# Attention value rows turned by VectorE from a DRAM copy, in pairs of tiles, in place of TensorE transposes

## The chip, the cores and the metric

The kernel runs on one core of one Trainium2 chip. The metric is the device time in microseconds of one execution; lower is better. A run is timed from outside; the profile of one execution gives the span of its instructions, which is a little shorter.

## The reference, cut to what matters

One encoder layer for two groups of streams: one new stream of 16 meta and 256 prompt tokens, and eight running streams of 16 tokens each, which have a cache of 256 past keys and values. That makes 400 token columns, and the kernel keeps all three groups (sample tokens, prompt tokens, meta tokens) in one matrix of them.

```
aq, ak, av, mq, mk, mv, mi, mf, mo = split(rms_norm(x) @ w_in)    # 2048 -> 56 tiles of 128 columns
s   = q @ k^T * DQK**-0.5 + relative bias, masked by chunk       # two maps per head, 4 heads
w   = softmax(s[0]) - lam * softmax(s[1])
o   = rms_norm(w @ v, subln_g)                                    # v: new rows and, for a stream, the cached ones
hm  = chunkwise mLSTM of mq, mk, mv with states C, n, m
x   = x + concat(o, hm * sigmoid(mo)) @ w_out
y   = x + square(relu(rms_norm(x) @ w_up)) @ w_down
```

Outputs are y, the new keys (`k_prompt`, `k_sample`), the new values (`v_prompt`, `v_sample`) and the new mLSTM states. All arithmetic is fp32; the large products are made of three fp32r products each (weights and activations split in a high and a low part).

## The kernel before

**Tiles of the projections.** The first product is done in tiles of 128 output columns, numbered t = 0 to 47. In each the 2048 inputs are summed in 16 steps, four in a quarter q = 0 to 3, and each step is three matmuls over the 400 (or 384) token columns: activation high by weight high (L540), low by high (L541), high by low (L542). A quarter is 12 matmuls. SyncE loads raw weights two half tiles at a time (`load_tile`), ScalarE copies a quarter into `w_hi` (L511), VectorE subtracts it into `w_lo` (L520), and TensorE waits for `w_lo`. There are four quarter buffers, so these two engines are at most a tile ahead of TensorE. Behind each tile VectorE reads the sum from `acc` and scales it (`scaled`, L1440). Tiles 0 to 7 are queries, 8 to 15 keys, 16 to 23 the attention's values (`av`, into `m1`, features on the partitions), 24 to 31 the mLSTM's queries and keys, 32 to 47 its values and gates.

**What runs beside them.** Every engine's program is written out tile by tile, and after each quarter it does the side work that a plan gives to that slot. `att_plan` makes the plan of the attention; slot s = 4·(t − 24) + q stands behind quarter q of tile t. All engines walk through the same plan, each doing its part of a step: `scores` (TensorE's products, then VectorE's row maximum, L1631), `exp` (ScalarE), `weights` (VectorE), `turn` (TensorE), `out`, and so on. The steps are, for each of four heads or stream pairs j, two query blocks of the prompt, ("p", j, 0) and ("p", j, 1), and the pair j of running streams. A prompt step begins at slot 4 + 8·(2j + i); the pair's last scores come at slot 16, 32, 48, 64.

**The key tiles of the streams.** The cached keys of stream b come in by strided loads (`load_keys`, `kc`), and VectorE turns them in four pieces into `kT` (L1702) at slots 4 + 8b to 7 + 8b. TensorE's `first_scores` (at slot 8 for stream 0) waits for the fourth piece, and so do its scores at slot 16 for stream 1 (`blocks_turned`).

**The new keys for the output.** `ko` (at slots 1, 5, 9, ..., 29) turns a tile of new keys in two VectorE transposes (L1679, L1681), and ScalarE issues four stores of it in the slots behind (`ko_store`).

**The value rows, which the change is about.** The attention needs `v` with tokens on the partitions (`av_rows`). At quarter 0 of tile t (18 to 23) and at slots 0 and 4, `turn_av` makes four TensorE transposes of an `m1` tile into a PSUM bank (L2177), and VectorE copies them out, the 128 x 384 part (L1599) and the 16 rows of the tail (L1600). That is eight times 4 transposes and 2 copies.

**GpSimd's queue.** GpSimd issues, in this order: the cached values of streams 0 and 1 (`load_values`, into the two buffers of `vc`); 16 loads of mLSTM state blocks through DRAM, each waiting for the next tile to have been scaled (`state_blocks`); the stores of the value rows to the outputs, after all eight tiles are turned; then the cached values of streams 2 to 7, in twos, each two behind the `out` step of the pair before; then the mLSTM's value blocks (`load_v_blocks`, 13 DMAs per head into `kv_blk`, in pieces of 32 x 32 that VectorE then transposes), and more. TensorE's `out` step of pair 0 (slot 20) waits for the cached values of both its streams.

## Time and profile before

| | us |
|---|---|
| median of 3 runs | 1732.14 (1731.73 to 1732.16) |
| the profiled execution's own time | 1731.3 |
| its span | 1729.5 |

```profile
PE 1723.6 (100%) x8450; PEld 1467.3 (85%) x8450; DVE 906.2 (52%) x1681; ACT 654.3 (38%) x1224; POOL 392.1 (23%) x558
PE   9999999999999999999999999999999999999999
DVE  5634676556687666545433554343465334456333
DMA  7685469999898676665334565344556444556542
q0 software_dynamic: 24976, 66.98, 14.4%
```

The first line gives each engine's busy time, its share of the span and its instructions (PE is TensorE's matmuls, PEld its weight loads, DVE is VectorE, ACT ScalarE, POOL GpSimd). The next three cut the span into 40 slices of 43 us and give the busy share in tenths: TensorE is busy throughout, VectorE about half, and the DMA engines are near full in slices 7 to 13, some 260 to 560 us, where the attention and the mLSTM run. The last one is GpSimd's DMA queue (packets, MB, share of the 16 DMA engines). TensorE's granted clock is 0.9 or more of full speed in every slice.

### The profile page before, as it was taken

The numbers are of one execution on the slowest core, as the hardware profiler recorded it, in microseconds if no ns is written. First come the engines' busy times: TensorE is split into PE (matmuls) and PEld (weight loads), VectorE is DVE, ScalarE is ACT, GpSimd is POOL, SyncE is SP. The second block draws the span as 40 slices with busy tenths as digits, with TensorE's granted clock in tenths as the row PEclk, the third lists the DMA queues.
The fourth block names the chain that finished last, engine by engine and source line by source line (L and its number), as shares of the span: only waits on it lengthen the run. The fifth ranks groups of instructions, "written<-read, shape, count | busy, mean of one in ns | idle before, by whom it ended". The sixth has DMA issues, their size and how long they took to land.

```text
span 1729.5 us, 24656 instructions
## 1 busy us (share of the span) xinstructions
PE 1723.6 (100%) x8450; PEld 1467.3 (85%) x8450; DVE 906.2 (52%) x1681; ACT 654.3 (38%) x1224; POOL 392.1 (23%) x558
## 2 busy tenths in 40 slices
PE   9999999999999999999999999999999999999999
PEld 8999999999997788888888888888888888888887
DVE  5634676556687666545433554343465334456333
ACT  5323754444354444333333333323333332333332
POOL 3321010002351253434000343000343100234100
PEclk9999999999999999999999999999999999999999
DMA  7685469999898676665334565344556444556542
GB/s 192 175 194 144 130 143 243 214 204 229 224 269 268 156 215 199 179 182 166 126 123 133 161 177 186 122 128 128 159 166 182 140 132 121 162 166 171 172 144 97
DMA packets 295746, 295.08 MB, mean 171 GB/s; under 512 B 97004, under 2 KB 202540, under 8 KB 295644
## 3 DMA queue, kind: packets, MB, share of 16 engines
q1 hardware_dynamic: 255606, 222.91, 46.7%
q0 software_dynamic: 24976, 66.98, 14.4%
q10 hardware_dynamic: 15062, 3.86, 1.1%
q8 instruction: 61, 1.00, 0.2%
q14 instruction: 41, 0.34, 0.1%
HBM read 261.44 MB, written 38.01 MB: 173 GB/s over the span
## 4 chain that ended last, share of the span: by engine, by line
PE 98%; DVE 1%; DMA 0%; issue 0%; ACT 0%; ACTq 0%; DVEq 0%
PE bank L680 9%; PE bank L681 9%; PE bank L639 9%; PE bank L638 9%; PE bank L640 9%; PE bank L679 9%; PE acc L540 8%; PE acc L541 8%; PE acc L542 8%; PE bank L2072 3%; PE ssb L638 2%; PE ssb L639 2%; PE ssb L640 2%; PE ssb L679 2%; PE ssb L680 2%; PE ssb L681 2%
## 5 line engine op out<-in xcount | busy, mean ns | idle before, releaser
L520 DVE TENSOR_TENSOR w_lo<-raw,w_hi 128x512 fp32r<-128x512 f32 x768 | 537.0, 705 | 753.8 <-ACT w_hi L511 753.2
L511 ACT ACTIVATE w_hi<-raw 128x512 fp32r<-128x512 f32 x768 | 482.4, 631 | 958.3 <-PE acc L542 195.5
L540 PE MATMUL acc<-a_hi,w_hi 128*128 128x400 f32 (+1 forms) x768 | 267.9, 349 | 0.2 <-DVE w_lo L520 0.2
L541 PE MATMUL acc<-a_lo,w_hi 128*128 128x400 f32 (+1 forms) x768 | 262.9, 342 | 0.0
L542 PE MATMUL acc<-a_hi,w_lo 128*128 128x400 f32 (+1 forms) x768 | 262.3, 342 | 0.0
L680 PE MATMUL bank<-w_lo,a_hi 128*128 128x512 f32 x640 | 253.0, 395 | 0.0
L681 PE MATMUL bank<-w_hi,a_lo 128*128 128x512 f32 x640 | 252.6, 395 | 0.0
L639 PE MATMUL bank<-w_lo,x2g_hi 128*128 128x512 f32 x640 | 252.4, 394 | 0.0
L640 PE MATMUL bank<-w_hi,x2g_lo 128*128 128x512 f32 x640 | 252.2, 394 | 0.0
L638 PE MATMUL bank<-w_hi,x2g_hi 128*128 128x512 f32 x640 | 252.1, 394 | 0.0
L679 PE MATMUL bank<-w_hi,a_hi 128*128 128x512 f32 x640 | 252.1, 394 | 0.0
L619 POOL DMA_DIRECT2D u_turned<-m x192 | 124.0, 653 | 550.1 <-DVE m L2015 548.6
L540 PEld LDWEIGHTS acc<-a_hi,w_hi 128*128 128x128 f32 x768 | 144.2, 188 | 4.8 <-issue 3.4
L542 PEld LDWEIGHTS acc<-a_hi,w_lo 128*128 128x128 f32 x768 | 144.8, 189 | 0.0
L541 PEld LDWEIGHTS acc<-a_lo,w_hi 128*128 128x128 f32 x768 | 144.3, 188 | 0.3
L681 PEld LDWEIGHTS bank<-w_hi,a_lo 128*128 128x128 f32 x640 | 120.7, 189 | 27.7
L640 PEld LDWEIGHTS bank<-w_hi,x2g_lo 128*128 128x128 f32 x640 | 120.5, 188 | 27.8
L680 PEld LDWEIGHTS bank<-w_lo,a_hi 128*128 128x128 f32 x640 | 120.4, 188 | 28.0
L679 PEld LDWEIGHTS bank<-w_hi,a_hi 128*128 128x128 f32 x640 | 120.4, 188 | 27.7
L639 PEld LDWEIGHTS bank<-w_lo,x2g_hi 128*128 128x128 f32 x640 | 120.3, 188 | 27.6
L638 PEld LDWEIGHTS bank<-w_hi,x2g_hi 128*128 128x128 f32 x640 | 120.3, 188 | 27.6 <-issue 0.2
L932 POOL TENSOR_TENSOR a_lo<-stage,a_hi 128x384 fp32r<-128x384 f32 x64 | 71.8, 1153 | 121.2 <-ACT a_hi L1347 121.2
(358 smaller groups left out, 1812.1 us busy)
## 6 DMA issues: line engine op xcount, KB each, us to landing
raw<-in_w_up SPq DMA_DIRECT2D x128, 512.0 KB, 3.8
raw<-in_w_down SPq DMA_DIRECT2D x128, 512.0 KB, 3.8
raw<-in_w_in SPq DMA_DIRECT2D x94, 512.0 KB, 4.9
raw<-in_w_out SPq DMA_DIRECT2D x32, 512.0 KB, 5.6
u_turned<-m POOLq DMA_DIRECT2D x192, 64.0 KB, 3.0
stage<-u_turned POOLq DMA_DIRECT2D x16, 768.0 KB, 6.2
vc<-in_cache_v POOLq DMA_DIRECT2D x32, 256.0 KB, 7.1
kc<-in_cache_k SPq DMA_DIRECT2D x128, 64.0 KB, 3.2
```

What stands on the lines that cost most here:

```text
L511: e.activation(w_hi[:, q], raw[:, slot, 4 * (q % 2):4 * (q % 2) + 4, :], ACT.Copy).then_inc(hi_ready, 1)
L520: e.tensor_tensor(w_lo[:, q], raw[:, slot, 4 * (q % 2):4 * (q % 2) + 4, :], w_hi[:, q].bitcast(F32), ALU.subtract).then_inc(lo_ready, 1)
L540: e.matmul(out, w_hi[:, q, kk], hi[:, k, at], start=k == 0, stop=False, skip_group_check=True)
L541: e.matmul(out, w_hi[:, q, kk], lo[:, k, at], start=False, stop=False, skip_group_check=True)
L542: last = e.matmul(out, w_lo[:, q, kk], hi[:, k, at], start=False, stop=k == KT - 1, skip_group_check=True)
L619: e.dma_start(bass.AP(tensor=u_turned_d.tensor, offset=(b % 2) * 4 * P * 3 * P + Y_STARTS[r] - META + 32 * a, ap=[[3 * P, 32], [32 * 3 * P ...
L638: e.matmul(to, x2g_hi[:, k, rows], hi_w, start=k == 0, stop=False, skip_group_check=True)
L639: e.matmul(to, x2g_hi[:, k, rows], lo_w, start=False, stop=False, skip_group_check=True)
L640: last = e.matmul(to, x2g_lo[:, k, rows], hi_w, start=False, stop=k == KT - 1, skip_group_check=True)
L679: e.matmul(out, a_hi[:, k, rows], hi_w, start=k == 0, stop=False, skip_group_check=True)
L680: e.matmul(out, a_hi[:, k, rows], lo_w, start=False, stop=False, skip_group_check=True)
L681: last = e.matmul(out, a_lo[:, k, rows], hi_w, start=False, stop=k == KT - 1, skip_group_check=True)
```

## The change

1. The TensorE transposes of the value tiles and VectorE's copies of them out of PSUM are gone. GpSimd stores each `m1` value tile to a DRAM tensor `av_d`, and after two of them `av_back` loads the pair back with 13 DMAs, in pieces of 32 features x 8 x 32 tokens, into the second buffer of `vc`, which is renamed `av_blk` for the purpose and has room for two pairs' halves (n % 2). VectorE then makes token rows of a pair by two transposes of 32 x 32 blocks (`turn_av`). The four pairs are turned behind quarter 1 of tiles 21 and 23, and at slots 3 and 14.
2. The cached values of stream 1 are loaded into that buffer only when all four pairs are turned, and the stores of the value rows go behind the loads of all streams.
3. The new keys are turned and stored every 6 slots, not every 4.
4. Some semaphores are shared between waits (`gw_padded` becomes `consts`, and the like); the waits remain as they were.

```
-AV_AHEAD = T_M - T_AV - 2
+KEYS_EVERY = 6
+AV_TURNS = {(5, 1): 0, (7, 1): 1}
...
-    plan += [(4 * (j - AV_AHEAD), "av", j) for j in range(AV_AHEAD, 8)] + [(4 * j + 1, "ko", j) for j in range(8)]
-    plan += [(4 * j + 2 + g, "ko_store", (j, g)) for j in range(8) for g in range(4)]
+    plan += [(3, "av", 2), (14, "av", 3)] + [(KEYS_EVERY * j + 1, "ko", j) for j in range(8)]
+    plan += [(KEYS_EVERY * j + 2 + g, "ko_store", (j, g)) for j in range(8) for g in range(4)]
...
+        av_d = nc.dram_tensor("av_d", [8, P, TOK], F32).ap()
...
+            av_blk = vc[:, 1].rearrange("p x (r i t) -> p x r i t", i=8, t=32)
...
-            for b in range(2):
-                load_values(b)
+            load_values(0)
+            e.memset(av_blk[0:32, :, 3, :, TAIL:32], 0.0).then_inc(S("wt_padded"), 1)
...
+            def av_back(n):
+                e.wait_ge(S("av_out"), 16 * 2 * (n + 1))
+                if n >= 2:
+                    e.wait_ge(S("av_turned"), n - 1)
+                else:
+                    e.wait_ge(S("wt_padded"), 2)
+                at = 2 * n * P * TOK
+                for j in range(4):
+                    rows = slice(32 * j, 32 * j + 32)
+                    for r in range(3):
+                        dma(av_blk[rows, n % 2, r], bass.AP(tensor=av_d.tensor, offset=at + STARTS[r] + 32 * j,
+                                                            ap=[[TOK, 32], [32 * TOK, 8], [1, 32]]), f"av_in{n % 2}")
+                dma(av_blk[0:32, n % 2, 3, :, 0:TAIL], ...)
...
             for n in range(16):
                 ... state_blocks as before ...
+                if n >= 8:
+                    if n > 8:
+                        e.wait_ge(S("av_out"), 16 * (n - 8))
+                    dma(av_d[n - 8], m1[:, n - 8], "av_out")
+                if n in (10, 12, 14, 15):
+                    av_back((n - 9) // 2)
-            read_out(e, *[("av", j) for j in range(8)])
+            e.wait_ge(S("av_turned"), 4)
+            load_values(1)
+            for b in range(2, BD):
+                done(e, ("o", b // 2 - 1))
+                load_values(b)
             ... the three stores of av_rows ...
-            for b in range(2, BD):
-                done(e, ("o", b // 2 - 1))
-                load_values(b)
...
-            def take_av(n):
-                b = take(e, ("av", n))
-                cs = slice(n * P, (n + 1) * P)
-                e.tensor_copy(av_rows[:, 0:3, cs], b[:, 0:3 * P].rearrange("p (r n) -> p r n", n=P))
-                taken(e.tensor_copy(av_rows[0:TAIL, 3, cs], b[0:TAIL, 3 * P:4 * P]), ("av", n))
+            def turn_av(n):
+                cs = slice(n * DV, (n + 1) * DV)
+                e.wait_ge(S(f"av_in{n % 2}"), 16 * 13 * (n // 2 + 1))
+                e.transpose(av_rows[0:32, 3, cs], av_blk[0:32, n % 2, 3].rearrange("p i t -> p (i t)"))
+                e.transpose(av_rows[:, 0:3, cs],
+                            av_blk[:, n % 2, 0:3].rearrange("p r i t -> p r (i t)")).then_inc(S("av_turned"), 1)
...
-            def turn_av(n):
-                e.wait_ge(acc_free, T_AV + n + 1)
-                turn_rows(("av", n), m1[:, n])
```

VectorE's program from the scaling of the last value tile (`m`, tile 23) to the first prompt step's scores (slots 0 to 4), before:

```order
L1440 TENSOR_TENSOR m<-acc,rstd_x 128x400
L520 TENSOR_TENSOR w_lo<-raw,w_hi 128x512
L1599 COPY av_rows<-bank 128x3x128
L1600 COPY av_rows<-bank 16x128
L520 TENSOR_TENSOR w_lo<-raw,w_hi 128x512
L1684 MEMSET w_new 128x128
L1685 MEMSET q_pad 128x8x16
L1679 STREAM_TRANSPOSE ko<-zt 128x288
L1681 STREAM_TRANSPOSE ko<-zt 128x128
L520 TENSOR_TENSOR w_lo<-raw,w_hi 128x512 x2
L1440 TENSOR_TENSOR m<-acc,rstd_x 128x384
L520 TENSOR_TENSOR w_lo<-raw,w_hi 128x512
```

Two more copies of `av_rows` follow there, and then the scores (L1631). The same stretch in the changed kernel, where L519 is the `w_lo` line, L1462 the scaling, L1621 and L1622 the transposes of `turn_av`, L1654 the scores:

```order
L1462 TENSOR_TENSOR m<-acc,rstd_x 128x400
L519 TENSOR_TENSOR w_lo<-raw,w_hi 128x512 x2
L1707 MEMSET w_new 128x128
L1708 MEMSET q_pad 128x8x16
L1702 STREAM_TRANSPOSE ko<-zt 128x288
L1704 STREAM_TRANSPOSE ko<-zt 128x128
L519 TENSOR_TENSOR w_lo<-raw,w_hi 128x512 x2
L1462 TENSOR_TENSOR m<-acc,rstd_x 128x384
L1621 STREAM_TRANSPOSE av_rows<-vc 32x256
L1622 STREAM_TRANSPOSE av_rows<-vc 128x3x256
L519 TENSOR_TENSOR w_lo<-raw,w_hi 128x512
L1654 ISA s_sb,smx<-bank,bias_p 128x144
```

Four copies have left this stretch and two transposes, of a pair, have come, ahead of the last `w_lo`. VectorE at slots 12 to 15 of the changed kernel, where the key tiles of stream 1 are turned (L1725 is `kT`; before, the same rows stand there without the two of `av_rows`):

```order
L1725 STREAM_TRANSPOSE kT<-kc 128x2x8x32
L519 TENSOR_TENSOR w_lo<-raw,w_hi 128x512
L1702 STREAM_TRANSPOSE ko<-zt 128x288
L1704 STREAM_TRANSPOSE ko<-zt 128x128
L1725 STREAM_TRANSPOSE kT<-kc 128x2x8x32
L519 TENSOR_TENSOR w_lo<-raw,w_hi 128x512
L1621 STREAM_TRANSPOSE av_rows<-vc 32x256
L1622 STREAM_TRANSPOSE av_rows<-vc 128x3x256
L1725 STREAM_TRANSPOSE kT<-kc 128x2x8x32
```

The pair's two transposes stand between the second and the third key piece. GpSimd's DMAs of the changed kernel from the last stores of value tiles on:

```order
L728 DMA state_blocks<-in_state_C 32x64x32
L728 DMA av_d<-m 128x400
L728 DMA vc<-av_d 32x8x32 x12
L728 DMA vc<-av_d 32x8x16
L728 DMA state_blocks<-in_state_C 32x64x32
L728 DMA av_d<-m 128x400
L728 DMA vc<-av_d 32x8x32 x12
L728 DMA vc<-av_d 32x8x16
L728 DMA vc<-in_cache_v 32x2x1024 x28
L728 DMA out<-av_rows 128x1024
```

The first four rows are the reload of the third pair (tiles 4 and 5), behind the store of tile 6; before, only the two rows of `state_blocks` stood there, and `out<-av_rows` came right behind them.

## Rows read from the trace of the kernel before

**Rows 1.** The page: the chain of waits that ended last, by engine
```profile
PE 98%; DVE 1%; DMA 0%; issue 0%; ACT 0%; ACTq 0%; DVEq 0%
```
**Rows 2.** TensorE's waits: line, for whom, us in total, times, longest
```profile
PE bank L2072 <- DVE kT L1702: 0.4, 1, 0.4
```
**Rows 3.** Timeline of TensorE at tile 18: start us, us, line, operation [idle before]
```profile
184.90 0.34 PE L542 MATMUL acc<-a_hi,w_lo 128*128 128x400 f32 x1
185.08 0.60 PE L2177 MATMUL bank<-ident,m 128*128 128x128 f32 x4
...
185.71 0.34 PE L541 MATMUL acc<-a_lo,w_hi 128*128 128x400 f32 x1
185.89 0.35 PE L542 MATMUL acc<-a_hi,w_lo 128*128 128x400 f32 x1
```
**Rows 4.** The transposes' line L2177: ns min/median/max, first and last start
```profile
L2177 PE MATMUL bank<-ident,m x32: 270/272/273, 185.1 to 253.7; 128*128 128x128 f32 x24, 128*16 128x128 f32 x8
```
**Rows 5.** Timeline of VectorE from the scaling of tile 22 to slot 8
```profile
239.09 0.57 DVE L1440 TENSOR_TENSOR m<-acc,rstd_x 128x400 f32<-128x400 f32 x1
...
254.65 0.68 DVE L520 TENSOR_TENSOR w_lo<-raw,w_hi 128x512 fp32r<-128x512 f32 x1
255.25 0.55 DVE L1599 COPY av_rows<-bank 128x384 f32<-128x384 f32 x1
...
255.91 0.28 DVE L1631 CUSTOM_DVE_ANT_0 s_sb<-bank,bias_p 128x144 f32<-128x144 f32 x1
...
260.03 0.47 DVE L1679 STREAM_TRANSPOSE ko<-zt 128x288 f32<-128x288 f32 x1
...
260.61 0.67 DVE L1702 STREAM_TRANSPOSE kT<-kc 128x512 f32<-128x512 f32 x1
...
263.57 0.70 DVE L1702 STREAM_TRANSPOSE kT<-kc 128x512 f32<-128x512 f32 x1
```
**Rows 6.** Timeline of TensorE at slot 8
```profile
262.94 1.02 PE L2072 MATMUL ssb<-av_rows,wT 128*128 128x256 f32 x4
264.32 0.64 PE L2072 MATMUL bank<-kT,q_pad 128*32 128x256 f32 x8 [0.36 <-DVE kT L1702]
```
**Rows 7.** Tile kv_blk: instructions with ns min/median/max, and time to landing
```profile
L729 POOL DMA_DIRECT2D kv_blk<-kv_d x52: 615/618/667, 420.2 to 519.2; - x52
L1916 DVE STREAM_TRANSPOSE kv_rows<-kv_blk x4: 556/558/559, 449.0 to 556.4; 32x384 f32<-32x384 f32 x4
L1917 DVE STREAM_TRANSPOSE kv_rows<-kv_blk x4: 1323/1323/1323, 449.5 to 556.9; 128x1152 f32<-128x1152 f32 x4
...
DMA to landing us min/median/max: 2.5/5.6/10.1
```
**Rows 8.** Timeline of GpSimd: the state blocks behind tile 22
```profile
240.24 1.05 POOL L729 DMA_DIRECT2D state_blocks<-in_state_C  x1 [9.16 <-DVE m L1440]
```
**Rows 9.** Tile state_blocks: time to landing of its DMAs
```profile
DMA to landing us min/median/max: 4.0/4.6/9.7
```
**Rows 10.** Timeline of VectorE at slots 12 to 15, stream 1
```profile
278.01 0.17 DVE L1641 RECIPROCAL smx<-smx 128x2 f32<-128x2 f32 x1 [1.19 <-ACT s_sb L1187]
...
284.01 0.71 DVE L1702 STREAM_TRANSPOSE kT<-kc 128x512 f32<-128x512 f32 x1
```
**Rows 11.** Timeline of TensorE at slots 16 and 20
```profile
285.33 1.07 PE L2072 MATMUL bank<-kT,q_pad 128*32 128x256 f32 x16
...
295.81 1.93 PE L2072 MATMUL ssb<-vc,wT 128*32 128x256 f32 x32
```
**Rows 12.** Tile vc: time to landing of the cached values' DMAs
```profile
DMA to landing us min/median/max: 4.2/7.1/11.0
```
**Rows 13.** Timeline of VectorE at slot 38, stream 4
```profile
349.70 0.69 DVE L520 TENSOR_TENSOR w_lo<-raw,w_hi 128x512 fp32r<-128x512 f32 x1 [0.44 <-ACT w_hi L511]
```
**Rows 14.** The page's DMA issues: KB each, us to landing
```profile
out<-av_rows POOLq DMA_DIRECT2D x1, 1024.0 KB, 9.1
```

More of the change, by code:

```diff
@@ L249, in plan_banks @@
     for _, what, n in ATT_PLAN:
-        if what == "av":
-            u.add(("av", n), (2, 4)[n % 2])
-        elif what == "first_scores":
+        if what == "first_scores":
             u.add(("s", STEPS[n], 0), 0)
@@ L1192, in att_work @@
                         if n == 0:
-                            e.wait_ge(S("wt_padded"), 2)
+                            e.wait_ge(S("wt_padded"), 3)
                         if is_pair(step):
@@ L1570, in qk_norm @@
                 cols = pair_cols(u)
-                if q == 0 and u >= 2:
-                    take_av(u - 2)
+                if (u, q) in AV_TURNS:
+                    turn_av(AV_TURNS[u, q])
                 elif q == 2 and u + 1 < 8:
@@ L1673, in att_work @@
                     if what == "av":
-                        take_av(n)
+                        turn_av(n)
                     elif what == "ko":
@@ L1683, in att_work @@
                     elif what == "mask":
-                        e.memset(w_new[:], 0.0).then_inc(S("w_new_zero"), 1)
-                        e.memset(q_pad[:, :, 1], 0.0).then_inc(S("w_new_zero"), 1)
-                        e.wait_ge(S("w_new_zero"), 2)
-                        e.wait_ge(S("bias_masked"), 2)
-                        e.wait_ge(S("lam_ready"), 1)
+                        e.memset(w_new[:], 0.0).then_inc(S("pads_zero"), 1)
+                        e.memset(q_pad[:, :, 1], 0.0).then_inc(S("pads_zero"), 1)
+                        e.wait_ge(S("pads_zero"), 2)
+                        e.wait_ge(S("bias_masked"), 3)
+                        e.wait_ge(S("lam_prod"), 2)
                     elif what == "key_blocks":
@@ L1883, in enter @@
                 e.memset(expo[:, EXPO_TAIL:], 0.0).then_inc(S("pads_zero"), 1)
-                e.wait_ge(S("pads_zero"), 3)
+                e.wait_ge(S("pads_zero"), 5)
                 e.memset(v_rows[:, 0:3, DV:DVX], 1.0)
@@ L1895, in enter @@
                     last = ts(swm[:, h], bmask[:], cols[:, 1, 0, h:h + 1], None, ALU.mult)
-                last.then_inc(S("swm_made"), 1)
-                e.wait_ge(S("swm_made"), 1)
+                last.then_inc(S("seq_paired"), 1)
+                e.wait_ge(S("seq_paired"), 3)
                 read_out(e, "nT")
@@ L2158, in qk_sums @@
                 u = t - T_AV
-                if q == 0 and u >= 2:
-                    turn_av(u - 2)
-                elif q == 1:
+                if q == 1:
                     if u == 0:
-                        e.wait_ge(S("consts"), 4)
+                        e.wait_ge(S("consts"), 5)
                     e.wait_ge(S("n_low"), u + 1)
@@ L2251, in att_work @@
                     yield slot
-                    if what == "av":
-                        turn_av(n)
-                    elif what == "first_scores":
+                    if what == "first_scores":
                         first_scores(STEPS[n])
```

14 lines of the change are left out of this document (7 added, 7 removed).

## Prediction

> **What bounds the kernel now.** I read the page first: the chain that ended last is TensorE's for 98% of the span [rows 1]. So TensorE sets the end, and every other engine matters only where TensorE waits for it. Then the table of TensorE's waits: in the stretch that the change touches it has one entry, 0.4 us for the key tiles that VectorE turns [rows 2]. The timeline shows where: at slot 8 TensorE has done its products with the value rows at 262.94, and could go on with stream 0's keys, but the fourth key piece begins on VectorE at 263.57 and takes 0.70, so TensorE begins at 264.32 after 0.36 of idling [rows 5, 6]. What TensorE gives up is thus worth its full length, provided that nothing then comes too late for it.
>
> **What TensorE loses.** The weight matmuls follow each other at 0.18 us (185.71 to 185.89). From 184.90 to 185.71 stand one turn of four transposes and two such steps: 0.81 − 0.36 = 0.45 us a turn, switching back to the weight products included [rows 3]. Eight turns go: −3.6 us. A transpose by itself lasts 272 ns [rows 4], but most of that overlaps the next one. The Trainium skill, "TensorE: Matmul & The Clock Gate", Part 4: PE-mode transpose, gives about 275 ns for one in a kernel's context, and the trace agrees on that length; counted by it, 32 transposes would be 32 × 275 ns = 8.8 us, an estimate from that page. Start to start they cost 0.45 us for four, and that is what I sum.
>
> **VectorE, slots 0 to 4.** Here the stretch from the scaling of tile 23 to slot 8 is almost one block of VectorE work. Two takes go, each 0.66 us (255.25 to 255.91) [rows 5]: −1.32. One turn of a pair comes, 128 x 768 and 32 x 256 elements. Neither is in the trace. Nearest are 128 x 512 at 0.70 [rows 5] and 128 x 1152 at 1.32, and for the small one 32 x 384 at 0.56 [rows 7]; a line through the first two gives 0.95 for 768, the small one in proportion 0.4, less 0.1 of overlap between neighbours: 1.25. Its bounds are 0.9 (the 0.70 and half of the 0.56, overlapping) and 1.88 (both upper rows). VectorE's work is then 0.07 us shorter, but TensorE arrives 2 × 0.45 = 0.9 earlier, as it has two turns less (slots 0 and 4). The fourth key piece is late already, so all of the difference is waited: +0.8 us. The `ko` that moves from slot 5 to slot 7 (0.58 us, 260.03 to 260.61) [rows 5] stays ahead of that piece and changes nothing there.
>
> **The new wait at slot 3.** VectorE now waits for the reload of value tiles 4 and 5. Queued behind this wait are a `w_lo`, the first prompt step's scores and weights, and all four key pieces of stream 0, on which TensorE waits. GpSimd's issue of the state blocks behind tile 22 stands at 240.24 and takes 1.05 [rows 8]; one store, taken as 0.62 like a reload DMA, and 13 reloads at 0.618 [rows 7] follow. The last one is issued at 240.24 + 1.05 + 0.62 + 12 × 0.618 = 249.3. Landing took 2.5 to 10.1 with a median of 5.6 for the like pieces of `kv_blk` [rows 7], and 4.0 to 9.7 with 4.6 for the state blocks in this stretch [rows 9]. I take 5.1, between the medians: 254.4. VectorE would be there at 254.65 − 0.66 (tile 6's take is gone) − 0.45 (TensorE has one turn less since tile 22) = 253.5. The wait is 0.9 us; with the ends 2.5 and 10.1 it is 0 or 5.9. As the fourth key piece has no spare, TensorE pays it whole: +0.9. Tile 0 to 3's reloads are issued at least as early against quarter 1 of tiles 21 and 23, some 20 us after their issue begins, and cost nothing unless landings are double the longest seen. The fourth pair has until slot 14, over 20 us after its issue.
>
> A rule of the Trainium skill speaks against the reload: "DMA: Bandwidth & Descriptors", Specifications, wants at least 512 B a transfer and says that smaller ones are read, modified and written. The reload is in pieces of 128 B, as `kv_blk` is, so the landings of rows 7 have that price in them already; by the rule the reload sits nearer the late end.
>
> **VectorE, slots 12 to 15.** The fourth pair is turned between stream 1's key pieces. VectorE works without a pause from 278.01, where ScalarE frees it, to the end of the fourth piece at 284.01 + 0.71 = 284.72 [rows 10]. TensorE needs that at 285.33 [rows 11], and between the end of such a piece and its use lie 0.05 (264.27 to 264.32) [rows 5, 6]. So 0.56 are to spare and 1.25 come: +0.7 us (0.3 to 1.3 by the bounds of the turn). A `ko` stands at slot 13 in both versions.
>
> **What costs nothing, and under what cover.** The values of stream 1 are issued when VectorE has done the fourth pair, about 283.5; the last of four issues at some 0.53 is at 285.1, landing takes 7.1 in the median and 11.0 at most [rows 12], so 292.2 or 296.1, and the product begins at 295.81 [rows 11], a little later with the waits above. Spare: 3.6 us, −0.3 in the worst case. The `ko` that is now at slot 37 adds 0.58 to stream 4's pieces, but VectorE idles 0.44 for ScalarE behind it [rows 13]; the rest fits into the like of the 0.56 found for stream 1. The reloads keep GpSimd from its next state blocks by 8 us, three times; no one waits for these before slot 67. The early removal of four `vc` DMAs and of six other turns' copies frees VectorE and the DMA engines where TensorE waits for neither: 0. The stores of the value rows now stand behind stream 7's values; 9.1 us to landing [rows 14], and VectorE asks for them only at slot 67, over 30 us later. The renamed semaphores: 0.
>
> **Sum.** −3.6 + 0.8 + 0.9 + 0.7 = −1.2 us. The profiled execution took 1731.3, so 1730.1; the median stands 0.84 above it, which gives 1730.9.
>
> **The rivals.**
> - *No new wait.* If the reload lands at the early end and VectorE has slack that I don't see in slots 0 to 4 and 12 to 15, only −3.6 remains: 1728.5. For it: TensorE waits almost nowhere now. Against: the 0.36 of rows 6 show a late VectorE, and rows 10 and 11 leave 0.56 for 1.25.
> - *The reload is late, slower than before.* At slot 3 VectorE stands until the third pair has landed; at 10.1 us of landing that is 5.9 instead of 0.9. −3.6 + 0.8 + 5.9 + 0.7 = +3.8: 1735.9. It makes the kernel slower than before from a wait of 2.1 us on, a landing of 6.3. For it: at this time the key loads of stream 0 and `state_blocks` share the DMA engines, and one of the latter took 9.7. Against: in the stretch's medians it is 4.6.
> - *The value stores get in the way.* They now fall on the key loads of stream 7. If these are pushed back by half of the stores' 9.1 us, and all of that is waited for, +4.5: 1735.4. Against: stream 7's pieces are turned some 25 us after the stores start.
> - *The transposes are worth their length.* By the rows' 272 ns each, 32 × 0.272 = 8.7 in place of 3.6: 1725.8. Against: rows 3, start to start. This is what the page's 275 ns would give.
>
> **Chances.** My forecast 0.60 (own range 1729.6 to 1732.5), no new wait 0.18, reload late 0.12, stores 0.07, transposes worth their length 0.03. About 0.2%, 3.5 us, is what a measurement of this kernel can tell from no change, so faster means below 1728.7 and slower above 1735.6. No new wait is just at that line, and I count most of it as faster: 0.13 + 0.03 and a little of the forecast's tail, 0.18. Slower is half of the late reload and a part of the stores: 0.11. The same: 0.71. The range 1728.3 to 1734.6 reaches from "no new wait" into the late reload up to a wait of 4.6 us.
>
> **What would show it.** In the changed profile TensorE's line for value transposes is gone and a tile of 400 columns with quarter sums is 0.45 us shorter. TensorE waits for `kT` twice: about 2.1 us at slot 8 (0.4 + 0.8 + 0.9) and 0.7 at slot 16. VectorE's `av_rows` transposes take 0.95 and 0.4, and at slot 3 the line has about 0.9 us of idle time before it with the reload as its releaser. TensorE's `vc` products have no wait. A `kT` wait under 1 us in all would make it the first rival; one of 6 the second; a wait in the 400s the third; anything above 0.1 us for `w_lo` would be a cost that I have not seen.

## The result, and the profile after

| | us, median (lowest to highest, runs) | ratio, 95% interval |
|---|---|---|
| before | 1731.99 (1731.15 to 1732.36, 19) | |
| after | 1734.70 (1732.01 to 1736.70, 19) | 1.0016 (1.0009 to 1.0022) |
| predicted | 1730.9, range 1728.3 to 1734.6 | |

The forecast was 3.8 us too low, and the time lies just above its range. Two things are to be explained: the median, and a spread of 4.7 us where the kernel before had 1.2. The profiled execution took 1732.04 us, so it is one of the shortest, and doesn't show all of the loss. Its chain of waits, against [rows 1]:

```profile
PE 95%; DVE 2%; SPq 1%; issue 1%; ACT 0%; DMA 0%; ACTq 0%; POOL 0%; DVEq 0%; POOLq 0%
```

TensorE's waits, against [rows 2] (line, for whom, us in total, times, longest):

```profile
PE bank L2095 <- DVE kT L1725: 1.7, 2, 1.0
PE bank L637 <- issue: 1.4, 1, 1.4
PE bank L2102 <- ACT o_rows L1247: 0.6, 1, 0.6
```

The tile that answers to [rows 3] no longer has its step of 0.45 us (TensorE at tile 18; start us, us):

```profile
184.66 0.35 PE L539 MATMUL acc<-a_hi,w_hi 128*128 128x400 f32 x1
184.84 0.35 PE L540 MATMUL acc<-a_lo,w_hi 128*128 128x400 f32 x1
185.03 0.34 PE L541 MATMUL acc<-a_hi,w_lo 128*128 128x400 f32 x1
```

VectorE's turn of a pair, which no row of before showed, at slot 3, and its last key piece of stream 1, against [rows 5, 10]:

```profile
251.97 0.42 DVE L1621 STREAM_TRANSPOSE av_rows<-vc 32x256 f32<-32x256 f32 x1
252.33 0.92 DVE L1622 STREAM_TRANSPOSE av_rows<-vc 128x768 f32<-128x768 f32 x1
253.19 0.64 DVE L519 TENSOR_TENSOR w_lo<-raw,w_hi 128x512 fp32r<-128x512 f32 x1
...
282.93 0.69 DVE L1725 STREAM_TRANSPOSE kT<-kc 128x512 f32<-128x512 f32 x1
```

TensorE at slots 8 and 16, against [rows 6, 11]:

```profile
262.10 0.64 PE L2095 MATMUL bank<-kT,q_pad 128*32 128x256 f32 x8 [1.02 <-DVE kT L1725]
...
283.77 0.85 PE L2095 MATMUL bank<-kT,q_pad 128*32 128x256 f32 x12 [0.64 <-DVE kT L1725]
```

And the time to landing of the tile `vc`, now with the 52 reload transfers in it, against [rows 7, 9, 12]:

```profile
DMA to landing us min/median/max: 2.4/5.0/10.8
```

From these alone the kernel would be faster. To see where a lead is won or lost I set the start of one and the same product of TensorE (counted back from the last one) in each trace against the kernel before. Minus is ahead, plus behind. At 170 us nothing has been changed yet; what stands there is the difference between two executions.

```
us in the kernel before   170    258    300    417    432   1185   1300
after                    0.68  -2.87  -1.55  -1.55  -0.73  -0.80   0.74
```

So 3.55 us are won by 258 us and 1.32 given back at the two waits for `kT`. 0.82 go between 417 and 432 us, at the wait for `o_rows`, and 1.54 at 1191 us, where the last big loop jumps back. The prediction had neither of the last two. Every table of leads below is made in this way; a lead is that of one execution, so it is to be read beside the median.

### The profile page after: what moved, and what is told of

It reads as the page before. It is cut to its first block, busy times and chain, and to the rows that moved or that the text cites. A ratio compares the mean times of both kernels' runs of the same rounds, so it can differ in the third digit from the quotient of the medians.

```text
span 1730.2 us, 24637 instructions
## 1 busy us (share of the span) xinstructions
PE 1721.5 (99%) x8418; PEld 1464.6 (85%) x8418; DVE 905.8 (52%) x1673; ACT 653.3 (38%) x1224; POOL 426.2 (25%) x619
## 4 chain that ended last, share of the span: by engine, by line
PE 95%; DVE 2%; SPq 1%; issue 1%; ACT 0%; DMA 0%; ACTq 0%; POOL 0%; DVEq 0%; POOLq 0%
PE bank L679 9%; PE bank L680 9%; PE bank L638 9%; PE bank L637 9%; PE bank L639 9%; PE bank L678 9%; PE acc L539 7%; PE acc L540 7%; PE acc L541 7%; PE bank L2095 3%; PE ssb L637 2%; PE ssb L638 2%; PE ssb L639 2%; PE ssb L678 2%; PE ssb L679 2%; PE ssb L680 2%
## 5 line engine op out<-in xcount | busy, mean ns | idle before, releaser
L519 DVE TENSOR_TENSOR w_lo<-raw,w_hi 128x512 fp32r<-128x512 f32 x768 | 537.1, 705 | 756.8 <-ACT w_hi L510 753.4
```

What stands on the lines that cost most here:

```text
L519: e.tensor_tensor(w_lo[:, q], raw[:, slot, 4 * (q % 2):4 * (q % 2) + 4, :], w_hi[:, q].bitcast(F32), ALU.subtract).then_inc(lo_ready, 1)
```

## Experiments

Each kernel ran 11 times, and the kernel before 21 or 33 times beside each set of kernels (medians 1731.64 to 1731.96). The ratio is to that. These theories stood in turn: F, fetching of instructions at the jump back; W and P, TensorE's own waits or its lead; K, the spacing of the new keys' stores, or the waits for `kT`; S, the transfers that the change adds or moves into the stage from 240 to 430 us.

**1. The changed kernel again, and the place of the loop.** `a_again` is the changed kernel itself.

> The changed kernel once more, to see in the trace what one of its usual, longer executions holds; the profiled one before was among its shortest (1732.0 us, where the median is 1734.7). Theory F (fetch of instructions at TensorE's jump back in the last big loop): the first product of that loop's second turn comes late by 1.5 us and more, and the difference between executions is there. Theory W (waits in the attention stage): the two waits for kT (0.7 us each) and the wait for o_rows at 426 us are longer or more than in the first profile. Both: a median near 1734.7 us with a spread of 4 us.

1732.65 us (1730.23 to 1735.36), 1.0005 (0.9996 to 1.0014).

```
# a_pad72, behind each tile of T_AV to T_M - 1
+                for _ in range(9):
+                    e.nop()
# a_slot0 (slot 0, changed kernel) and b_slot184 (slot 184, kernel before)
-            with e.Fori(1, GROUPS - 1) as g:
+            with nc.Fori(1, GROUPS - 1, engines=[e.engine], head_slot={e.engine: 0}) as g:
```

> The changed kernel with 9 instructions that do nothing on TensorE after each of tiles T_AV to T_M - 1, 72 in all, so that everything behind them, the last big loop too, lies where it lay in the kernel before. Theory F: the loss in the loop is gone; what is left is -3.6 us for the turns, +1.4 for the two waits for kT and +0.7 at 426 us: about 1730.5 us, with a spread of 1 us as before. Theory W: nothing changes, near 1734.7 us with a spread of 4 us.

1733.95 us (1730.52 to 1738.04), 1.0011 (1.0002 to 1.0020). TensorE's instruction records number 9414, as in the changed kernel, and no trace of this case has a record of an instruction that does nothing. So it is not shown that the padding was executed, and this may be the changed code a third time. Either way its loop loses only 0.2 us, and the 1730.5 us that Theory F asks for then did not come.

> The changed kernel with TensorE's last big loop laid so that its first instruction is the first of a block of 256 that is fetched at once. Theory F: as with the padding, about 1730.5 us and a narrow spread, if the place of the loop's head alone decides. Theory W: near 1734.7 us.

1733.54 us (1731.34 to 1735.55), 1.0007 (0.9998 to 1.0016).

> The kernel before with TensorE's last big loop laid so that its first instruction is number 184 of a block of 256, where it lies in the changed kernel (72 instructions ahead of a boundary); nothing else is changed. Theory F: 1 to 5 us slower than the kernel before, with a spread of some 4 us. Theory W: as the kernel before, 1732.0 us.

1733.39 us (1731.60 to 1733.93), 1.0006 (0.9997 to 1.0015).

```
us in the kernel before   170    258    300    417    432   1185   1300
a_again                  0.46  -3.08  -1.70  -1.70   0.84   1.41   1.35
a_pad72                  0.20  -3.35  -2.03  -2.03   2.46   2.45   2.65
a_slot0                  0.15  -3.39  -2.01  -0.77   4.03   4.22   4.26
b_slot184                0.46   0.46   0.41   0.41   0.41   0.49   2.20
```

The part up to 300 us repeats to 0.2 us. The part from 300 to 432 doesn't: in four executions with the changed kernel's work it cost 0.8, 2.5, 4.5 and 6.0 us. That is the spread. The loop costs 1.7 us in `b_slot184`, and nothing in `a_again`, which is the same code as the profiled one that lost 1.5 there. In `b_slot184` the median rose with it, by 1.4 us. Theory F names a true loss, but not the main one. One more thing is to be kept in mind: the changed code itself gave medians of 1734.70 and 1732.65, 2.05 us apart. `a_again` shows what happens around 417 us. SyncE's issues, first of the kernel before, then of `a_again` (start us, us that the issue took):

```profile
393.29 0.37 SPq L488 DMA_DIRECT2D raw<-in_w_in  x1
393.70 11.56 SPq L1002 DMA_DIRECT2D kc<-in_cache_k  x8
405.31 0.49 SPq L488 DMA_DIRECT2D raw<-in_w_in  x1
405.85 6.26 SPq L1002 DMA_DIRECT2D kc<-in_cache_k  x8
412.16 0.49 SPq L980 DMA_DIRECT2D kv_d<-stage  x1
412.76 1.13 SPq L488 DMA_DIRECT2D raw<-in_w_in  x2
```

```profile
391.65 0.37 SPq L487 DMA_DIRECT2D raw<-in_w_in  x1
392.07 17.23 SPq L1024 DMA_DIRECT2D kc<-in_cache_k  x8
409.35 0.48 SPq L487 DMA_DIRECT2D raw<-in_w_in  x1
409.88 6.12 SPq L1024 DMA_DIRECT2D kc<-in_cache_k  x8
416.04 0.49 SPq L1002 DMA_DIRECT2D kv_d<-stage  x1
416.64 1.14 SPq L487 DMA_DIRECT2D raw<-in_w_in  x2
```

GpSimd loads streams 6 and 7's values just ahead of it, and now stores the value rows too (`a_again`):

```profile
387.81 3.63 POOL L728 DMA_DIRECT2D vc<-in_cache_v  x7 [0.23 <-issue]
391.43 1.81 POOL L728 DMA_DIRECT2D out<-av_rows  x3
```

Eight key issues take 17.2 us instead of 11.6, and the weight pieces queued behind them on SyncE come 4 us later. ScalarE waits for them, in the kernel before never, here (all waits from 240 to 440 us, then one of them, then TensorE behind it):

```profile
ACT w_hi L510 <- DMA raw<-in_w_in: 16.8, 6, 5.3
```
```profile
421.71 0.63 ACT L510 ACTIVATE w_hi<-raw 128x512 fp32r<-128x512 f32 x1 [5.32 <-DMA raw<-in_w_in]
```
```profile
428.79 0.44 PE L2102 MATMUL bank<-ident,o_rows 128*128 128x128 f32 x2 [1.46 <-ACT o_rows L1247]
```

The `o_rows` scaling stands behind that `w_hi` on ScalarE. So the wait is named after `o_rows`, but its cause is a late weight piece.

**2. The value stores and the spacing of the key stores.**

```
# a_early (b_late is the reverse move in the kernel before)
             load_values(1)
+            dma(v_sample..., av_rows[:, 0], "v_stored")        # and the two for vp
             for b in range(2, BD):
                 done(e, ("o", b // 2 - 1))
                 load_values(b)
-            dma(v_sample..., av_rows[:, 0], "v_stored")        # and the two for vp
# a_keys4
-KEYS_EVERY = 6
+KEYS_EVERY = 4
# a_early_turns: as a_early, and
-    plan += [(3, "av", 2), (14, "av", 3)] + ...
+    plan += [(9, "av", 2), (11, "av", 3)] + ...
```

> The changed kernel with the three stores of value rows issued ahead of the loads of streams 2 to 7 (some 283 us) and no more behind them (392 us); nothing else is changed. In four executions of the changed code the stretch from 417 to 432 us cost 0.8, 2.5, 4.5 and 4.8 us more than in the kernel before. Theory S (the stores behind stream 7's values hold up the weight and key loads that SP issues at the same time): that loss goes; what is left is what the changed kernel had gained at 400 us, 1.6 to 2.0 us, so about 1730.2 us, with a spread of 1 to 2 us from the jump back in the last big loop. Theory K (the wider spacing of new keys' stores, or the two waits for kT): nothing changes, 1732.6 to 1734.7 us with a spread of 4 us.

1734.26 us (1731.97 to 1737.24), 1.0014 (1.0005 to 1.0023).

> The kernel before with only the value rows' stores moved behind the loads of streams 2 to 7; TensorE still turns the values and VectorE copies them. Theory S: a loss of 1 to 5 us between 417 and 432 us, and the wider spread: 1733 to 1736 us. Theory K: 1732.0 us as before.

1731.67 us (1731.30 to 1732.78), 0.9999 (0.9990 to 1.0008).

> The changed kernel with new keys' stores at every fourth slot as before (KEYS_EVERY 4); the value stores stay behind the loads. Theory S: the loss from 417 to 432 us stays, 1732.6 to 1734.7 us. Theory K: the spacing of these stores was the cause, about 1730.5 us and a spread of 1 us.

1734.17 us (1731.45 to 1738.50), 1.0017 (1.0007 to 1.0026).

> As the first kernel of this call, and the turns of pairs 2 and 3 at slots 9 and 11 and no longer at 3 and 14, so that neither stands ahead of key blocks of streams 0 and 1 on VectorE. If the two waits for kT (0.7 us each above the kernel before) come from these turns: both go, and the time is 1.4 us below the first kernel's, about 1728.8 us. If they come from late key loads, they stay, at about 1730.2 us.

1735.66 us (1733.97 to 1738.20), 1.0021 (1.0012 to 1.0030).

```
us in the kernel before   170    258    300    417    432   1185   1300
a_early                 -0.06  -3.61  -2.30   4.74   4.74   4.71   4.90
b_late                   0.50   0.50   0.38   0.38   0.38   0.66   0.58
a_keys4                  0.53  -3.02  -1.71  -1.71   0.29   0.25   0.15
a_early_turns            0.80  -2.74   2.29   2.29   3.97   4.04   4.04
```

By the medians Theory S had failed twice. The leads of `a_early` say otherwise. With the stores at 283 us nothing is lost from 417 to 432, as expected; but 7.0 us are lost behind them, all of it between 300 and 320 us. With the stores some 8 us earlier still, 5.0 us are lost between 258 and 300. So a loss goes where the stores go; but `a_early_turns` also loses 1.7 us from 417 to 432, where it has no stores. `b_late` loses nothing there: its eight key issues take 14.07 us instead of 11.56, and the weight piece behind them lands just as it is wanted, so the stores alone use up the room that there is and no more. The spacing of the key stores is not needed for it: with the old spacing the loss at 432 stays. `a_early_turns` has no wait of 1 us at slot 8 any more (0.2 us for `kT` in all), so the turns at slots 3 and 14 do cause those waits.

**3. Stores left out, stores in a gap, and the rest of the change alone.**

```
# a_nostore (a_nostore_turns: and turns at slots 9 and 11)
-            dma(v_sample..., av_rows[:, 0], "v_stored")
+            dma(v_sample...[0:1], av_rows[0:1, 0], "v_stored") # likewise one row of each vp
# a_383_turns: turns at 9 and 11, stores inside the loop over b
+                if b == 6:
+                    e.wait_ge(S("blocks_turned"), 25)
+                    dma(v_sample..., av_rows[:, 0], "v_stored")    # and the two for vp
# b_rest (kernel before)
-            for b in range(2):
-                load_values(b)
+            load_values(0)
...
             read_out(e, *[("av", j) for j in range(8)])
+            load_values(1)                                     # value stores behind the loop
# ... and "ko" and "ko_store" at 6 * j for 4 * j
```

> The changed kernel without its value output: of the three stores of value rows one row each is left, at their place behind the loads of streams 2 to 7. Theory S (these 1.1 MB beside 2 MB of values, 1 MB of keys and the weights make the transfers of 387 to 416 us too long): SP's keys from 392 us take 18 us again as in the kernel before, and no more 22 to 24, the loss from 417 to 432 us is gone, and the time is 1730.0 us with a spread of 1 to 2. Theory P (TensorE, 2 us earlier, is too early for the transfers in any case): the loss stays at 1 us and more, 1732 us and up.

1731.21 us (1728.97 to 1732.70), 0.9995 (0.9986 to 1.0004).

> As the first of this call, with the turns of pairs 2 and 3 at slots 9 and 11. With early stores these turns took away the waits for kT (ledger at 270 us: 3.0 us ahead and not 2.4), but the stores then came at 275 us and the next stretch lost 5 us. If the stores alone did that, this one is 1.4 us below the first of this call: 1728.6 us. If the earlier load of stream 1's values does it (it follows the last turn), it loses some 3 us between 270 and 300 us: 1733 us.

1731.02 us (1729.15 to 1732.85), 0.9996 (0.9987 to 1.0005).

> The changed kernel with the whole value output stored at 383 us, in the gap between the keys of streams 5 and 6 and the values of stream 6 (GpSimd waits for the first key block of stream 6), and the turns of pairs 2 and 3 at slots 9 and 11. Theory S with room in that gap: within 1 us of the second kernel of this call. If the gap is too short (the values of stream 6 start 3 us later), the keys from 392 us take over 20 us again, and it is 2 to 4 us above that kernel.

1733.13 us (1731.14 to 1736.21), 1.0010 (1.0001 to 1.0019).

> The kernel before with all of the change but the way of the values: TensorE turns them and VectorE copies them as before; stream 1's values are loaded behind the last copy, new keys' stores stand at every sixth slot, and the value stores follow the loads of streams 2 to 7. Theory S: SP's keys from 392 us take 20 us and more, but TensorE doesn't wait, since here nothing has used up the slack of 1.9 us: 1732 us as before. If the order of transfers alone costs TensorE time: 1733 us and up, with a wide spread.

1732.11 us (1731.47 to 1733.54), 1.0002 (0.9993 to 1.0012).

```
us in the kernel before   170    258    300    417    432   1185   1300
a_nostore                0.64  -2.90  -1.57  -1.57  -1.57  -1.60  -1.69
a_nostore_turns          0.41  -3.13  -3.38  -2.61  -0.91  -0.93  -1.02
a_383_turns              0.45  -3.10  -3.40  -3.28  -0.08  -0.06  -0.14
b_rest                   0.45   0.45   0.34   0.34   2.09   2.01   2.25
```

Without the stores the loss of 417 to 432 is gone in the profile, and the median falls by 1.4 to 3.5 us against the changed kernel's three medians; the spread stays 3.7 us, and the profiled execution (1729.70 us) is 1.5 us below the median, so the others lose something that this trace doesn't show. With the turns at 9 and 11 the whole lead of 3.4 us reaches 300 us, but 2.5 us of it are lost by 432 even without stores. `b_rest` was the surprise: the kernel before, with TensorE as late as ever, loses 1.8 us by 432. This is its longest execution, though (1733.54 us); its median stands 0.4 us above that of the kernel before, which is no clear difference. The first eight of its sixteen key issues take 16.64 us, all sixteen reach from 394.0 to 416.7 us (in the kernel before from 393.7 to 412.1):

```profile
394.03 16.64 SPq L1002 DMA_DIRECT2D kc<-in_cache_k  x8
```

**4. The lead alone, and the added transfers alone.**

```
# b_noturns (kernel before): TensorE's turn_av goes, and in VectorE's take_av
-                b = take(e, ("av", n))
+                e.wait_ge(acc_free, T_AV + n + 1)
-                e.tensor_copy(av_rows[:, 0:3, cs], b[:, 0:3 * P]...)
+                e.tensor_copy(av_rows[:, 0:3, cs], m1[:, n, 0:3 * P]...)
# a_noreload (a_noreload_nostore: and the stores cut to one row each)
-                if n in (10, 12, 14, 15):
-                    av_back((n - 9) // 2)
             e.wait_ge(S("av_turned"), 4)
-            load_values(1)                                     # now behind load_values(0)
# ... and VectorE's turns wait for these values and for the stores to av_d
# a_noreload_v281: load_values(1) stays where it is, and the turns read a tile that is cleared
# a_split: stores as in a_383_turns, but v_sample's at b == 4 (blocks_turned 17); turns at 3 and 14
```

> The kernel before without TensorE's 32 transposes of the values; VectorE copies the same number of elements from the unturned tiles at the same places, so the values in the output and in the attention are not the reference's. No transfer is changed. Theory P (a lead of TensorE is lost at the weight pieces that land just in time, whatever the transfers): the lead of 3.6 us at 258 us shrinks to some 1.8 us by 330 or 420 us (the slack of before at tiles 33 and 41 is 1.8 and 1.9 us): 1730.1 us. Theory S (the pieces follow TensorE, and only added transfers make them late): the 3.6 us are kept, 1728.3 us, with a spread of 1 us.

1728.89 us (1728.43 to 1729.71), 0.9985 (0.9976 to 0.9994).

> The changed kernel without the 52 transfers that read the values back in blocks, and with stream 1's values loaded at the start, as before; VectorE turns what lies in that tile, so the values are not the reference's. Transfers that are left of the change: the stores of value tiles from 190 us, the spacing of new keys' stores, the value stores behind the loads. Theory S, shares added up: the wait for the weights at tile 33 goes (slack 1.8 us again), the one at tile 41 stays because of the value stores: some 1.5 us below the changed kernel, 1732 us. Theory P: as the changed kernel, 1733.5 us.

1730.84 us (1729.85 to 1732.45), 0.9994 (0.9985 to 1.0003).

> As the kernel before it in this call, and of the three value stores one row each is left. All that the change adds to the transfers from 240 to 420 us is gone. Theory S: 3.0 us and more of the lead are kept, less the 1.4 us that TensorE waits for kT: 1730.2 us with a spread of 1 us. Theory P: some 1731.2 us, as without the stores alone, with its spread of 4 us.

1729.81 us (1729.04 to 1730.39), 0.9989 (0.9980 to 0.9998).

> As a_noreload (the changed kernel without the 52 transfers that read the values back; 1730.8 us), but stream 1's values are loaded behind the last turn, near 281 us, as in the changed kernel. VectorE turns a cleared tile, so the values are not the reference's. If the reload alone took the room: 1730.8 us again. If the load at 281 us did: as the changed kernel, 1733 us and up. With both alike: about 1732 us.

1733.11 us (1730.65 to 1737.57), 1.0013 (1.0004 to 1.0022).

> The changed kernel, complete, with the value stores in two parts, each in a gap of SP's key loads: the sample rows at 340 us, the prompt rows at 383 us (GpSimd waits for the first key block of streams 4 and 6). Theory S with room in the gaps: as the kernel without the stores, 1731.2 us. If a store there only pushes the values of streams 4 and 6 into the key loads: 1733 us, as the kernel with all of it at 383 us.

1734.01 us (1731.90 to 1736.35), 1.0012 (1.0003 to 1.0021).

```
us in the kernel before   170    258    300    417    432   1185   1300
b_noturns                0.07  -3.48  -2.72  -2.73  -2.72  -2.49  -2.55
a_noreload               0.97  -2.58  -1.18  -1.18   0.10   1.24   1.16
a_noreload_nostore       0.40  -3.15  -1.84  -1.84  -1.84  -1.80  -1.51
a_noreload_v281          0.05  -3.50  -2.16  -2.16  -0.71  -0.71  -0.64
a_split                  0.77  -2.78  -1.42  -1.14   1.99   2.05   3.37
```

`b_noturns` decides between S and P: TensorE gets the same lead with no transfer changed, gives back 0.8 us at slot 8, keeps the other 2.7 through this stage and ends 2.55 ahead, and the kernel is 2.8 us faster with a spread of 1.3. Theory P falls. Its waits for the late key piece, against [rows 2, 6]:

```profile
PE ssb L2068 <- ACT wT L1205: 0.5, 1, 0.5
PE bank L2068 <- DVE kT L1698: 0.4, 1, 0.4
```

Taking the added transfers away brings the spread down step by step: 4.7 and 5.1 us in the changed kernel (7.5 in `a_pad72`), 2.6 without reload and with stream 1's values early, 1.35 without the stores as well. `a_noreload_v281` parts the first of these steps: with the reload gone but stream 1's values still at 281 us the median is 1733.1 again, 2.3 us above `a_noreload`. That is about as much as two medians of the changed code differ, so the size is rough; that the spread goes from 2.6 to 6.9 us with it says the same. So it seems to be less the reads of 128 bytes that cost, and more 1 MB of plain loads at a bad time. SyncE in `a_noreload`, then in `a_noreload_v281`:

```profile
285.06 6.19 SPq L1023 DMA_DIRECT2D kc<-in_cache_k  x8
291.29 2.55 SPq L487 DMA_DIRECT2D raw<-in_w_in  x2
...
302.27 11.57 SPq L1023 DMA_DIRECT2D kc<-in_cache_k  x8
```
```profile
285.14 9.63 SPq L1022 DMA_DIRECT2D kc<-in_cache_k  x8
294.82 1.12 SPq L487 DMA_DIRECT2D raw<-in_w_in  x2
...
301.29 13.82 SPq L1022 DMA_DIRECT2D kc<-in_cache_k  x8
```

The keys take 3.4 us longer, the two weight pieces are issued 3.5 us later, and so run into the 2 MB of values that GpSimd asks for at 296 us; the next keys take 2.3 us longer. How far ahead the pieces land shows where this ends (for the first half of a weight tile: us from landing to the start of `w_hi`, from the landing events; 0.02 is a piece that was waited for):

```
tile   before b_noturns a_noreload_nostore a_noreload a_noreload_v281 after a_again a_split
33      1.79    2.15         2.35             2.25         0.02        0.55   0.02    0.02
37      2.23    2.66         2.13             0.86         0.13        2.19   0.02    0.02
41      1.91    1.12         2.14             0.02         0.02        0.02   0.02    0.02
```

The kept traces join the two ends of this chain. Take in each the time of the eight key issues that begin near 392 us (in `a_early` at 398), and TensorE's loss from 417 to 432 us:

```
                     eight issues, us   loss, us
b_slot184                 10.2            0
a_half                    10.8            0
before                    11.6            -
a_noreload_nostore        11.9            0
a_early                   11.9            0
b_noturns                 12.6            0
a_nostore                 13.3            0
b_late                    14.1            0
after                     15.2            0.8
a_early_turns             15.2            1.7
a_nostore_turns           16.0            1.7
a_noreload                16.4            1.3
b_rest                    16.6            1.8
a_again                   17.2            2.5
a_pad72                   17.2            4.5
a_noreload_v281           17.3            1.5
a_split                   17.7            3.1
a_keys4                   17.8            2.0
a_383_turns               18.3            3.2
a_slot0                   20.6            4.8
```

Up to 14.1 us nothing is lost, from 15.2 us on always something. Neither the lead nor the value stores are needed for a loss (`b_rest`, `a_nostore_turns`), and neither does it alone (`b_noturns`, `b_late`).

`a_split` and `a_383_turns` did not test the gap that I had in mind: the wait for the key block let the stores go only at 346.4 and 391.9 us (`a_383_turns`: 389.7), right ahead of the values of streams 4 and 6, which they pushed back. ScalarE then waited 18.5 us for weights in `a_split`. Whether stores in a true gap (322 to 326, 340 to 345 us) cost less was not tried.

**5. A version that should keep half.** VectorE turns heads 0 and 1 by way of memory, TensorE turns tiles 4 to 7 as before; stores and key stores as before; stream 1's values behind the second turn.

```
# a_half (changed kernel)
-                if n in (10, 12, 14, 15):
+                if n in (10, 12):
                     av_back((n - 9) // 2)
+                if n == 13:
+                    e.wait_ge(S("av_turned"), 2)
+                    load_values(1)
# TensorE's turn and VectorE's take of tiles 4 to 7 as in the kernel before; KEYS_EVERY = 4
```

> A complete version made from both: heads 0 and 1 (value tiles 0 to 3) are stored, read back in blocks and turned by VectorE, which is done at 231 us, ahead of the key loads; TensorE turns tiles 4 to 7 as before. Stream 1's values are loaded at 232 us, the value stores come at 256 us and new keys' stores at every fourth slot, as in the kernel before. Theory S: no transfer is added between 240 and 430 us, so the lead of 4 x 0.45 = 1.8 us is kept, and the wait for kT is the 0.4 us of before: 1731.7 - 1.8 = 1729.9 us, with a spread of 1 us; faster than both. Theory P has fallen with b_noturns. If reads of 128 bytes at 200 and 221 us delay the state blocks or stream 0's keys instead: 1731.7 us and up.

1735.60 us (1733.22 to 1737.36), 1.0019 (1.0010 to 1.0028).

```
us in the kernel before   170    258    300    417    432   1185   1300
a_half                  -0.22  -2.02   1.37   1.37   1.37   1.80   5.69
```

1.80 us of lead at 258, as summed. Then 3.4 us are lost: I had put the second turn at 231 us, but quarter 1 of tile 23 is at 241, where stream 0's keys begin:

```profile
241.01 2.11 POOL L732 DMA_DIRECT2D vc<-in_cache_v  x4 [11.94 <-DVE av_rows L1630]
```
```profile
264.14 1.06 PE L2110 MATMUL bank<-kT,q_pad 128*32 128x256 f32 x8 [2.07 <-DVE kT L1740]
```

From 270 to 432 it then loses nothing, with the transfers of before in that stage. The miss fits Theory S, but what made this wait was not taken apart, and a gain did not come: no complete version that beats the kernel before was found. The other 3.9 us go at the jump back; the trace names a wait for 1.9 of them (below), and the rest is open.

## Why the prediction was wrong

**What TensorE loses, −3.6.** Right: 3.55 us between 170 and 258 us, and 3.5 to 3.6 in nearly every version without these turns. The rival by the length of a transpose (−8.7) is out, and with it the 275 ns of the Trainium skill ("TensorE: Matmul & The Clock Gate", Part 4: PE-mode transpose) as a price: the length is right (272 ns), the cost start to start is 0.44 for four.

**VectorE at slots 0 to 4, +0.8.** Right in kind and size: TensorE lost 0.6 between 258 and 270 us, and 0.8 in `b_noturns`, where the lead alone meets the late key piece. The turn takes 0.42 and 0.92, against 0.4 and 0.95.

**The new wait at slot 3, +0.9.** It was not there: the turn at 251.97 has no idle time before it. VectorE came 1.5 us earlier than summed (253.5), and the reload was in time all the same: its last transfer was issued at 246.9 us, not 249.3, and landed at 250.6, 3.7 us later and not 5.1.

**Slots 12 to 15, +0.7.** Right: 0.71. The wait for `kT` there is 0.64.

The three others give −2.1; the trace has −2.23 from 170 to 300 us. So up to 300 us the sum of −1.2 was right to 1.0 us, in the kernel's favour. The sum has no loss behind 300 us, and 1731.99 − 2.2 would have made 1729.8; the measured median is 4.9 us above that.

**What costs nothing, summed as 0.** This is the step that failed. I priced each moved transfer by its own landing against the moment when its own data are asked for: stream 1's values against their product, the value stores against slot 67. Both are in time, and TensorE never waits for a `vc` tile. What I left out is the work that shares the DMA engines and stands queued on SyncE: the key loads and, behind them, the weight pieces, which at tiles 33, 37 and 41 landed only 1.8, 2.2 and 1.9 us before use. TensorE lost 0.8 to 6.0 us from 300 to 432 us in four executions with the changed kernel's work, behind such pieces, and nothing where no transfer was changed (`b_noturns`). By medians, the value stores cost 1.0 us (1730.84 against 1729.81, nothing else added); stream 1's values at 281 us instead of the start, 2.3 us (1733.11 against 1730.84); the reload itself what the changed kernel's medians leave above 1733.11, −0.5 to 1.6 us. These shares are rough, since two medians of the same changed code lie 2.05 us apart, and they add up otherwise in another order: without the stores but with the rest the median is 1731.21. That transfers are the cause is shown; how it is divided among them is not.

**The rivals.** The third had the mechanism (the stores get in the way of stream 7's transfers), its size (+4.5; measured 0.8 to 6.0 at 432) and nearly the time, 1735.4; its sign, a wait in the 400s, is there. I gave it 0.07, because stream 7's keys had 25 us. What was late was the weight piece queued behind them. It is not the whole of it: a loss comes there without the stores too (`a_nostore_turns`). The late reload did not happen.

**The jump back, +1.5 in the profiled execution,** was in no term. It can come from where the loop's code lies, which the change shifts: laid there, the kernel before lost 1.4 us of median (`b_slot184`). But `a_again`, the same code, has none of it, and `a_noreload_nostore`, whose TensorE program is that of the changed kernel, has a median of 1729.81 us with a spread of 1.35, which leaves no room for such a loss in most executions. So it is a small part of the 4.9 us; why it comes in one execution and not in another is open.

## What to carry to other kernels

A transfer that is moved must be priced against what is queued beside and behind it, not against the use of its own data. Find, for the stage that it enters, the piece with the least time between landing and use (here weights with 1.8 us), and take that as the room that there is. When the median rises and the spread with it, compare where one and the same product stands in several executions: the part that repeats is the change's own work, the part that doesn't was, here, transfers in a stage where the DMA engines are busy all the time. And leave the work out first (as `b_noturns` did) to see what the idea is worth at most: 2.8 us here, of which no complete version kept any.

## What the runs showed of the hardware

**The DMA engines' share is near one before and after.** The share and GB/s (last two numbers) from 300 to 430 us, before and after:

```profile
300.00:430.00 130.00, 130.00 (x883) 120.80 (x882) 77.91 (x212) 56.98 (x171) 19.20 (x36) 1.00 0.98 217
```
```profile
300.00:430.00 130.00, 129.38 (x878) 119.66 (x876) 78.05 (x212) 55.57 (x167) 19.40 (x36) 1.00 1.00 229
```

The share was 0.98 before the change. Rows of this view belonged into the prediction, as a warning that added transfers may lengthen others. They don't give the price: the changed kernel moved 229 GB/s at 1.00, and `b_noturns` keeps its lead at 0.98.

**One issue in SyncE's queue can stand for long while GpSimd's transfers are moving.** GpSimd's 2 MB of values are under way at this time in the kernel before too, and there the longest of SyncE's eight key issues took 3.5 us, in `a_nostore` 4.1. With the value stores (1.6 MB in all, not the 1.1 MB of an expectation above) right behind the values the longest took 5.9 us in `a_again`, 7.1 in `b_late`, 7.9 in the changed kernel and 13.1 in `a_slot0`. But it also took 7.4 us in `a_nostore_turns` and 9.8 in `a_early_turns`, with no such stores there, so what sets the length is not shown.

**The jump back of TensorE's big loop.** At 1188 us, TensorE's sequencer ran its next instruction 3.5 us after the branch in the kernel before and 3.4 to 3.8 in `a_again`, `a_pad72`, `a_slot0` and `a_nostore`. It took 5.0 us in the profiled execution of the changed kernel and 5.1 in `b_slot184`. Beside it stand the packets of the instruction queue from 1185 to 1195.5 us, in the kernel before and in the changed one:

```profile
q8 instruction: 2, 0.03, 1.3%
```
```profile
q8 instruction: 3, 0.05, 2.9%
```

`b_slot184` has three as well, `a_again` two. Two of the three run side by side there, 1.9 to 2.2 us each, where the first one in other traces took 1.0 to 1.3. TensorE then idled (the first line, the changed kernel; the second, `a_half`, for another engine, VectorE, at the same place):

```profile
1193.20 0.50 PE L637 MATMUL bank<-w_hi,x2g_hi 128*128 128x512 f32 x1 [1.38 <-issue]
```
```profile
PE bank L641 <- DVE y_rows L2080: 1.9, 1, 1.9
```

The Trainium skill, "Runtime: NRT & Kernel Launch", Instruction fetch mechanics, says that a taken branch whose target is not in the window makes the engine fetch it before it goes on; the traces agree, with 3.4 to 5.1 us from branch to next instruction. What decides between one block and two stays open: it differed between two executions of the same code.
